# The order of the split products in a two-block fp32 network: first everything that needs the weights' high part, then what needs their low part

## What is computed

```python
u = jnp.einsum('bsd,de->bse', h, w_in)             # 1024 x 1024, pool mixer
g = jnp.einsum('bsd,df->bsf', h, w_gate)           # 1024 x 2816, and w_up
y = jnp.einsum('bsf,fd->bsd', silu(g) * u, w_down) # 2816 x 1024
z = h @ w_in[l]                                    # second block, both layers
k, v = jnp.split(m @ wkv, 2, axis=-1)              # memory of 256 tokens
x = x + rms_norm(jnp.square(relu(h @ mlp_w1[l])) @ mlp_w2[l], gain)
```

## Time and profile before

| | |
|---|---|
| Three runs | 4376.33, 4382.73, 4385.43 us (median 4382.73) |
| Profiled execution, span from first to last instruction | 4367.8 us (the page has no time outside of it) |
| PE busy | 3840.5 us (88%) in 17197 matmuls |
| PEld, DVE | 2982.5 us (68%), 1824.4 us (42%) |
| ACT, POOL | 1209.0 us (28%), 1263.9 us (29%) |
| Mean granted TensorE clock | 0.890 of full |
| Transfers | 292.42 MB, 67 GB/s on average |

### The profile page before, as it was taken

One profiled execution on the slowest core, in us unless ns is written; L12 is line 12 of the kernel. 1 busy time (PEld: TensorE's weight loads), 2 busy tenths in 40 slices (PEclk: granted clock), 3 DMA queues, 4 the chain that ended last, 5 costly groups with the idle time before them and its releaser, 6 DMA issues.

```text
span 4367.8 us, 49579 instructions
## 1 busy us (share of the span) xinstructions
PE 3840.5 (88%) x17197; PEld 2982.5 (68%) x17197; DVE 1824.4 (42%) x2706; ACT 1209.0 (28%) x1673; POOL 1263.9 (29%) x279
## 2 busy tenths in 40 slices
PE   5999998989997895887998899979678799898997
PEld 4788775557885653665877678858356587776886
DVE  4421424444125224664445461431456534636252
ACT  2332312333322211223333322221122333333221
POOL 2344531013543320002434134424000043422442
PEclk8999997569998985888999999989568799999998
DMA  2333320002332310001323123322000032312332
GB/s 97 96 87 105 87 87 29 0 28 80 95 94 71 107 59 1 1 1 49 106 87 116 39 87 97 96 76 89 2 1 1 16 108 89 105 59 68 97 96 67
DMA packets 384374, 292.42 MB, mean 67 GB/s; under 512 B 17737, under 2 KB 379683, under 8 KB 383688
## 3 DMA queue, kind: packets, MB, share of 16 engines
q1 hardware_dynamic: 375304, 285.67, 21.3%
q10 hardware_dynamic: 8896, 4.46, 0.4%
HBM read 286.92 MB, written 3.16 MB: 66 GB/s over the span
## 4 chain that ended last, share of the span: by engine, by line
PE 75%; DVE 10%; issue 7%; POOL 4%; ACT 3%; DMA 1%; DVEq 0%; SPq 0%; ACTq 0%; POOLq 0%
PE ps L453 19%; PE ps L457 18%; PE ps L456 18%; POOL w_lo L439 4%; PE ps L903 3%; PE ps L885 3%; PE ps L892 2%; PE ps L1326 1%; DVE y_f L1871 1%; PE ps L1320 1%; PE ps L1545 1%; PE ps L1536 1%; DVE acc L492 1%; PE ps L1543 1%; PE ps L1408 1%
## 5 line engine op out<-in xcount | busy, mean ns | idle before, releaser
L439 POOL TENSOR_TENSOR w_lo<-w_raw,w_hi 128x2048 fp32r<-128x2048 f32 x274 | 1263.5, 4611 | 3054.8 <-ACT w_hi L433 3054.8
L453 PE MATMUL ps<-h_hi,w_hi 128*128 128x512 f32 x2752 | 1088.3, 395 | 80.3 <-POOL w_lo L439 32.1
L456 PE MATMUL ps<-h_lo,w_hi 128*128 128x512 f32 x2752 | 1080.4, 393 | 0.0
L457 PE MATMUL ps<-h_hi,w_lo 128*128 128x512 f32 x2752 | 1079.7, 392 | 0.0
L433 ACT ACTIVATE w_hi<-w_raw 128x2048 fp32r<-128x2048 f32 x274 | 523.4, 1910 | 747.1 <-PE ps L453 683.9
L453 PEld LDWEIGHTS ps<-h_hi,w_hi 128*128 128x128 f32 x2752 | 521.5, 190 | 201.5 <-issue 51.1
L456 PEld LDWEIGHTS ps<-h_lo,w_hi 128*128 128x128 f32 x2752 | 521.8, 190 | 112.6 <-issue 2.1
L457 PEld LDWEIGHTS ps<-h_hi,w_lo 128*128 128x128 f32 x2752 | 520.7, 189 | 112.0
L453 PE MATMUL ps<-hid_hi,w_hi 128*128 128x512 f32 x864 | 338.4, 392 | 7.5 <-POOL w_lo L439 6.9
L456 PE MATMUL ps<-hid_lo,w_hi 128*128 128x512 f32 x864 | 336.3, 389 | 0.0
L457 PE MATMUL ps<-hid_hi,w_lo 128*128 128x512 f32 x864 | 336.3, 389 | 0.0
(11 more groups left out here) (364 smaller groups left out, 4850.7 us busy)
## 6 DMA issues: line engine op xcount, KB each, us to landing
w_raw<-mlp_w SPq DMA_DIRECT2D x128, 512.0 KB, 4.5
w_raw<-w_in SPq DMA_DIRECT2D x112, 512.0 KB, 4.5
w_raw<-ffn_w_gate SPq DMA_DIRECT2D x44, 512.0 KB, 4.0
w_raw<-ffn_w_up SPq DMA_DIRECT2D x44, 512.0 KB, 5.2
w_raw<-xa_wkv SPq DMA_DIRECT2D x32, 512.0 KB, 4.0
w_raw<-ffn_w_down SPq DMA_DIRECT2D x32, 384.0 KB, 3.8
w_raw<-attn_w_qkv SPq DMA_DIRECT2D x24, 512.0 KB, 4.1
w_raw<-ffn_w_down SPq DMA_DIRECT2D x32, 320.0 KB, 3.5
```

Of the source, the lines that this page charges most:

```text
L439: pool.tensor_tensor(w_lo[:, slot], w_raw[:, slot], w_hi[:, slot].bitcast(F32), ALU.subtract)\
L453: ins = pe.matmul(o, whi[:, kw, cols], rhi(kr), start=a == 0, stop=False)
L456: pe.matmul(o, whi[:, kw, cols], rlo(kr), start=False, stop=False)
L457: ins = pe.matmul(o, wlo[:, kw, cols], rhi(kr), start=False, stop=a == n - 1)
```

## The change

In `product` and `value_product` the low-weight matmuls move out of the loop into a second loop behind it. The first matmul of a chunk now waits for `hi_done` in place of `w_split`, and the wait for `w_split` stands ahead of the second loop of the chunk's first tile. The waits for `w_split` at the heads of the callers go away. SP's `load` waits for `w_split` of the chunk two before, in place of `chunk_begun`: what it must not overwrite, `w_raw`, is read for the last time by POOL.

```diff
-    for who, value in (("sp", -2), ("act", -1), ("pool", -1)):
+    for who, value in (("act", -1), ("pool", -1)):
         start(chunk_begun, who, value)
+    start(w_split, "sp", -2)
...
     def load(slot, *parts):
 
-        wait(sp, take(chunk_begun, "sp"))
+        wait(sp, take(w_split, "sp"))
...
         (whi, wlo), (rhi, rlo) = w, rhs
         n = len(kts)
+        if begin:
+            pe.wait_ge(*take(hi_done, "pe"))
         for a, (kw, kr) in enumerate(kts):
             if arrive is not None:
                 pe.wait_ge(*take(arrive, "pe"))
...
             pe.matmul(o, whi[:, kw, cols], rlo(kr), start=False, stop=False)
+        if begin:
+            pe.wait_ge(*take(w_split, "pe"))
+        for a, (kw, kr) in enumerate(kts):
             ins = pe.matmul(o, wlo[:, kw, cols], rhi(kr), start=False, stop=a == n - 1)
         return ins
...
     def pe_tiles(rhs, kt, c, slot, banks, free=bank_free, n=S, arrive=None):
 
-        pe.wait_ge(*take(w_split, "pe"))
         w = parts_of(slot, kt, c)
...
     def value_product(o, w, rhs, tok, begin):
 
         (whi, wlo), (rhi, rlo) = w, rhs
+        if begin:
+            pe.wait_ge(*take(hi_done, "pe"))
         for a in range(DT):
             ins = pe.matmul(o, rhi(a)[:, tok], whi[:, a, :], start=a == 0, stop=False)
             if begin and a == 0:
                 ins.then_inc(chunk_begun, 1)
-            pe.matmul(o, rhi(a)[:, tok], wlo[:, a, :], start=False, stop=False)
-            ins = pe.matmul(o, rlo(a)[:, tok], whi[:, a, :], start=False, stop=a == DT - 1)
+            pe.matmul(o, rlo(a)[:, tok], whi[:, a, :], start=False, stop=False)
+        if begin:
+            pe.wait_ge(*take(w_split, "pe"))
+        for a in range(DT):
+            ins = pe.matmul(o, rhi(a)[:, tok], wlo[:, a, :], start=False, stop=a == DT - 1)
         return ins
```

More of the change, by code:

```diff
@@ L593, in pool_pe @@
         for g in range(4):
-            if g % 2 == 0:
-                pe.wait_ge(*take(w_split, "pe"))
             for t in range(2):
```

## The result

| | before | changed |
|---|---|---|
| Median of 4 runs | 4379.53 us (4370.94 to 4385.43) | 4321.85 us (4303.08 to 4326.59) |
| Ratio of the two | | 0.9869, 95% interval 0.9841 to 0.9897 |
| Profiled execution: its time | about 4370 us (not recorded for before; see below) | 4318.56 us |
| Profiled execution: span | 4367.8 us | 4316.8 us |

The kernel got 58 us faster by the medians and 51.0 us by the spans of the two profiled executions, where 72 had been forecast. 4311 was forecast, and 4321.85 lies in the range. One run of e2_order_only took 16936.64 us, far from the usual state, and is left out of that kernel's median and ratio.

What follows compares the result with a forecast made beforehand. PE's matmuls set the time, standing 72.1 us for POOL's low part; 40 + 10 + 8 + 17 - 3.3 = 72 us off the 4367.8 us span gives 4296, plus 14.9 gives 4311 us (4293 to 4345).

Steps and rivals of the forecast that it cites:

- What bounds the kernel: Whole kernel: TensorE (PE) sets the time; its waits for POOL's low part total 72.1 us in 37 waits.
- Second chunks: Second chunk of a stage, seven windows 44.4 us too long by standing and lower clock; 4.5 stay, gain 40 us.
- Down projections: Down projections with 10 steps, two layers, each window 5.1 us too long; all goes, 10 us.
- Single waits: About ten waits elsewhere, such as 12-step projections and cross attention's queries; all find their high part ready, 8 us.
- Memory stages: The two memory stages: 3 + 1.8 + 2.3 + 1.5 = 8.6 us a stage, 17 us for both.
- 3 us is all that PE's earlier tiles can give back: First half of a memory stage: DVE waits for PE 1.10 and 1.87 us, so about 3 us can be gained.
- Rival B: DVE and POOL keep the memory stages (6 of 17 us come), lower clock stays behind short pauses; 4330 us, chance 0.12.
- Arrivals: First tiles taking activations one by one: cost 2.3 us at attention's output projection, 1 us for all others.
- Loads and waits: Earlier loads cost zero, since nobody waits for a load; the added waits, 274 in mid-tile, cost nothing.
- A: Each mid-tile wait costs a 0.11 us restart, 30 us in all, net gain 42: 4341 us, chance 0.13.
- C: The wait only moves: PE would stand in mid-tile as long as now; 4383 us, chance 0.03.
- D: Slower: the waiting weight load can't be prefetched, 0.38 us per chunk, 104 us against 72 gained; 4415 us, chance 0.05.

Runs made afterwards that it cites:

- e2_order_only: Changed kernel's order (low products behind high ones), but a chunk's first matmul waits for both high and low part, as before; 4374.98 us over nine runs, ratio 1.0011.
- e4: Changed kernel with loads waiting for both the low part of the chunk two before and that chunk's begin; 4316.39 us, ratio 0.9884.
- e9: On top of e5, ACT makes the second chunk's high part ahead of the norm's square root in the memory stages; 4295.77 us, ratio 0.9842.
- e6: Changed kernel with two satisfied waits ahead of the low products of every output tile, some 770 waits more; 4321.36 us, ratio 0.9891.
- e11: Changed kernel with four small clears on DVE ahead of the first copy, about 2 us; 4306.31 us, ratio 0.9857.
- e8: Kernel before without DVE's eight additions of squares in each memory stage, for reading the stage only; one run, 4382.86 us.
- e3: Kernel before with only the loads waiting for the low part of the chunk two before; 4368.87 us, ratio 0.9995.
- e5: Changed kernel, but first tiles that take activations one by one keep the old order and wait for both parts at their head; 4304.45 us, ratio 0.9865.
- e10: Kernel before with four small clears on DVE ahead of the first copy, about 2 us; 4373.20 us, ratio 1.0010.
- e1: Changed kernel unedited, timed once more beside the kernel before; 4316.88 us, ratio 0.9879.

## Why the prediction was right, point by point

**What bounds the kernel** held. PE sets the time, a steady chunk is 10.88 us in both kernels, and the low part was the largest thing that PE stood for.

**Second chunks: 40 us forecast, 39.3 measured.** Read as in the prediction, from the last matmul before the chunk to the start of the one after next, the seven places were 44.4 us too long and are 5.1 now: 1.04 at the first (12.15 against 11.11), 1.18 at its twin, 0.74 in the mixer input of the first layer, 2.13 in the second's and nothing at the three others. The lower clock went with the waits: all seven windows are at 1.00 now, where they had 0.82 to 0.90. Forecast for the first: low part at 188.1, 0.85 us left. Measured: 1.07 us between two matmuls at 187.28, of which 0.23 is their normal distance.

**Down projections: 10 us forecast, 10.2 measured** (46.14 and 46.13 became 41.03).

**Single waits: 8 us forecast, 7.7 measured,** added from the distances at the places named.

**Memory stages: 17 us forecast, 12.6 measured** (71.99 to 65.68 and 72.04 to 65.70). This is the term that was mis-sized. The step that failed is mainly the first half: "3 us is all that PE's earlier tiles can give back" counted DVE's two waits for PE as gain. From the stage's first chunk to the start of its fifth low part it was 44.3 us and is 42.8, so only 1.5 came; the second half gave 4.8 of the 5.6 forecast. In the trace after, DVE's tiles have no wait for PE left and DVE is at work without a pause, but each of its meetings with POOL takes 4.70 to 4.96 us, where those of before took 3.72 to 4.89. DVE in the changed kernel, same stage:

```profile
2270.40 4.96 DVE L1876 SCALAR_TENSOR_TENSOR y_f<-y_f,par,rstd 128x512 f32<-128x512 f32 x1
...
2277.05 0.75 DVE L1876 SCALAR_TENSOR_TENSOR y_f<-y_f,par,rstd 128x512 f32<-128x512 f32 x1
...
2279.49 4.92 DVE L1876 SCALAR_TENSOR_TENSOR y_f<-y_f,par,rstd 128x512 f32<-128x512 f32 x1
```

From one of the long ones to the next are 9.09 us, two tiles of DVE and one low part, and PE, with 5.8 us of work per chunk, stands again, now in mid-tile. Rival B had that mechanism (and the rule on the shared port pair of the Trainium skill, "SBUF — State Buffer", section "SBUF: two separate sides": the trace agrees, 4.96 against 0.75 us); its price for these stages, 6 us of 17, was too low. Its other half, that the lower clock would stay where a short pause is left, did not happen in the second chunks: their pauses in mid-tile are 0.45 to 0.76 us, and the clock is 1.00. In the memory stages it did happen in part. There 10 pauses of 1.59 to 2.63 us stand in mid-tile; behind four of the six that are longer than 2.5 us the granted clock of the next 2 us is 0.50 to 0.70, behind all others it is 1.00. PE behind the first and the third of them:

```profile
2265.76:2267.76 2.00, 2.00 (x10) 0.59 0.18 55
2283.92:2285.92 2.00, 2.00 (x16) 1.00 0.33 99
```

The pauses are 2.59 and 2.53 us long, so their length alone does not decide it.

**Arrivals: 3.3 us forecast, 1.6 measured, and 4.8 lost that are not arrivals.** The attention's output projection cost 1.6 us at the chunk named (2.3 forecast). The value chunks of the first block cost 1.5 and the output projections behind cross attention 1.5 and 1.8. At these three the pause ahead is as long as before, 0.90 and 2.54 us, but the matmuls behind it ran at the lower clock in the changed kernel; the forecast had no term for that. The value chunk's 13.01 us are 11.51 again in e4 and e9, which have the same order there. PE's first matmuls behind cross attention in the first layer, before:

```profile
2451.19 0.49 PE L453 MATMUL ps<-h_hi,w_hi 128*128 128x512 f32 x1 [2.54 <-DVE h_lo L1973]
2451.52 0.39 PE L456 MATMUL ps<-h_lo,w_hi 128*128 128x512 f32 x1
2451.75 0.40 PE L457 MATMUL ps<-h_hi,w_lo 128*128 128x512 f32 x1
```

and after:

```profile
2406.37 0.79 PE L456 MATMUL ps<-h_hi,w_hi 128*128 128x512 f32 x1 [2.54 <-DVE h_lo L1977]
2406.96 0.63 PE L459 MATMUL ps<-h_lo,w_hi 128*128 128x512 f32 x1
2407.38 0.63 PE L456 MATMUL ps<-h_hi,w_hi 128*128 128x512 f32 x1
```

0.42 us from start to start instead of 0.23. In e6 and e11 the first layer's stage is 66.7 and 67.0 us long, nearly the 66.65 of before, and in the changed kernel 68.2; e8, with the order of before, has 68.7. So this too is not tied to the change; why it falls one way or the other stays open.

**Loads and waits: zero forecast, zero measured** (e3, e4, e6), but for two readings. "Never for a transfer" overlooked two waits of ACT, for the first chunks of the pooling mixer and of the second block's first layer, 17.4 and 17.2 us before and 17.0 and 17.1 now; the change does not touch them. And "nobody waits for a load now, and nobody will" is wrong by 2.3 us in three waits of the memory stages, where POOL makes two low parts back to back and the load behind them is late. The first of them:

```profile
2307.44 1.92 ACT L434 ACTIVATE w_hi<-w_raw 128x2048 fp32r<-128x2048 f32 x1 [0.64 <-DMA w_raw<-xa_wkv]
```

The Trainium skill's 50 to 100 ns for a sequencer's reading of a semaphore ("Advanced Engine Details and Errata", section "Network/Comms") do not show up in PE's time, by e6. Rivals A, C and D are out: a steady chunk is at 10.88 us, and the waits in mid-tile add up to a third of the old ones.

**The time itself.** 72 us forecast against 63.7 in the dense stretches: 4.4 us of the difference are the memory stages, about 3 are that the costs were 6.4 us in place of 3.3, 4.8 of them matmuls at low clock behind unchanged pauses, and 1 is the other terms. The sum then went to the wrong base. I added 14.9 us for what lies around the span; the records of the changed kernel put 1.8 us around it (4318.56 against 4316.8). So the profiled execution of before, with its span of 4367.8, stands for about 4370 us by estimate, at the fast end of its runs, and the forecast from it should have been near 4298. That error of 13 us happened to meet the 13.5 us that the changed kernel lost in a sparse stretch in its first profile. The median of 4321.85 is so near 4311 partly by luck; the mechanism is shown by the table of distances and by e2 against the changed kernel, not by how near the median came.

## What to carry to other kernels

Where an operand is made in steps and the product needs the first step's result longer than the pipeline needs for the second, order the accumulation by what is ready and put the wait ahead of the terms that need it. Here a wait that was already satisfied cost nothing in mid-accumulation (e6), and a pause removed ahead of a burst gave back the slow first microseconds behind it as well (15.6 of 44.4 us). Where the other operand arrives slowly, piece by piece, the old order is better, by 1.5 us at one place here (e5), and in stages where two engines take turns expect only what these turns leave. Compare such kernels by distances between events in their dense stretches, since sparse stretches moved the total by some 15 us here, more than many changes are worth; and find out how far such a sum scatters before reading small differences from it.

## What the runs showed of the hardware that was not expected

The same 1618 matmuls between mixer input and merge took from 421.0 to 441.2 us, at granted clocks from 0.75 to 0.69, in kernels that differ only elsewhere. The same program moved by as much between runs (4303 to 4327 us), while the dense sum kept to 0.1 us in two profiles of it. In e10, with everything about 2 us later, one stretch was 6.8 us shorter than before, but the first profile and e1 differ by 10 us in each stretch with no edit at all, so the shift is not shown to be the cause. What decides how these stretches fall was not settled.

Behind pauses of nearly one length (2.53 to 2.63 us in the memory stages, 2.54 behind cross attention) the matmuls ran at the lower clock in some executions and places and at the upper one in others.
